# A hybrid decoder trunk on one core: gate and up matrices of the experts in runs of four rows a partition

## What is computed

```python
# mod = silu(c) @ ada_w + ada_b, split into sh1, sc1, g1, sh2, sc2, g2 (1024 channels each)
h = rmsnorm(x, norm2) * (1 + sc2) + sh2
x = x + g2 * hierarchical_moe(h, ...)

def expert_block(xb, e):            # xb: rows of h routed to expert e, of 32
    return (silu(xb @ w1[e]) * (xb @ w3[e])) @ w2[e]
# w1, w3 (gate and up): (32, 1024, 512); w2 (down): (32, 512, 1024)
```

## Time and profile before

| | us |
|---|---|
| median of 3 runs | 1860.86 |
| lowest, highest | 1858.2, 1867.57 |
| the profiled execution | 1862.04 |
| its span, first to last instruction | 1860.0 |
| PE busy in the span | 1669.9 (90%) |
| ACT, DVE busy | 411.1, 602.9 |
| first to last fetch of an expert's matrix issued | 1229.4 to 1799.7 |

### The profile page before, as it was taken

The page is one execution under the profiler, slowest core; times in us unless marked ns, Lnnn a source line. Parts: engine busy times, 40 slices in busy tenths (PEclk is TensorE's granted clock), DMA queues, the critical chain, the costliest instruction groups (busy, mean ns, idle before and its releaser), DMA issues. The chain is left out here.

```text
span 1860.0 us, 33711 instructions
## 1 busy us (share of the span) xinstructions
PE 1669.9 (90%) x14367; PEld 1118.3 (60%) x14367; DVE 602.9 (32%) x1534; ACT 411.1 (22%) x931; POOL 198.4 (11%) x228
## 2 busy tenths in 40 slices
PE   5999999998999979899999899828999988898892
PEld 3444446997777767544444345527777776677672
DVE  3523231004666656665564212260001000000002
ACT  4000000004666646301001011202212212121212
POOL 1205000000110110000000111111111111111110
PEclk9899999999999989999999999868999999999996
DMA  9873223401110044334432331159999999999995
GB/s 325 251 222 100 91 68 116 130 1 41 41 31 14 2 139 137 116 117 127 122 99 85 105 125 68 68 204 387 377 378 377 373 366 379 368 375 374 369 361 217
DMA packets 203953, 355.47 MB, mean 191 GB/s; under 512 B 14831, under 2 KB 94295, under 8 KB 203771
## 3 DMA queue, kind: packets, MB, share of 16 engines
q1 hardware_dynamic: 177264, 305.22, 46.1%
q0 software_dynamic: 13392, 27.93, 5.7%
q10 hardware_dynamic: 13148, 20.16, 3.1%
HBM read 321.29 MB, written 46.86 MB: 198 GB/s over the span
## 5 line engine op out<-in xcount | busy, mean ns | idle before, releaser
L2185 PE MATMUL psum<-sb_m_xT,sb_m_ring 128*64 128x64 f32 x4352 | 138.7, 225 | 30.1 <-issue 25.6
L2185 PEld LDWEIGHTS psum<-sb_m_xT,sb_m_ring 128*64 128x64 f32 x4352 | 134.2, 140 | 44.6 <-issue 44.6
L2180 PE MATMUL psum<-sb_m_xT,sb_m_ring 128*128 128x128 f32 x1152 | 135.9, 279 | 9.8 <-DMA sb_m_ring<-in_exp_w_dram 4.4
L2180 PEld LDWEIGHTS psum<-sb_m_xT,sb_m_ring 128*128 128x128 f32 x1152 | 133.2, 195 | 16.9 <-issue 10.7
L2113 DVE TENSOR_TENSOR sb_m_hT<-psum,sb_m_sg 128x128 f32<-128x128 f32 (+1 forms) x64 | 21.9, 341 | 368.4 <-ACT sb_m_sg L1959 368.4
L2193 PE MATMUL psum<-sb_m_ring,sb_m_hT 128*64 128x512 f32 (+1 forms) x416 | 129.0, 597 | 0.0
L1959 ACT ACTIVATE sb_m_sg<-psum 128x128 f32<-128x128 f32 (+1 forms) x64 | 20.3, 318 | 445.8 <-PE psum L2185 253.0
L1643 PE MATMUL psum<-sb_w_o_sb,sb_mT 128*128 128x512 f32 x256 | 113.2, 601 | 3.7 <-PEq L196 3.7
L711 PE MATMUL psum<-sb_vD,sb_room 128*128 128x512 f32 x240 | 104.6, 592 | 0.0
L1947 ACT ACTIVATE sb_m_xT<-psum,sb_mod,sb_modA 128x64 f32<-128x64 f32 (+1 forms) x256 | 84.4, 435 | 57.8 <-PE psum L2171 57.2
L962 ACT ACTIVATE sb_d_probs<-sb_d_probs,sb_d_nmax 128x640 f32<-128x640 f32 (+7 forms) x128 | 93.3, 736 | 4.9 <-DVE sb_d_nmax L1002 4.4
(11 more groups left out here) (304 smaller groups left out, 2319.7 us busy)
## 6 DMA issues: line engine op xcount, KB each, us to landing
sb_m_ring<-in_exp_w_dram SPq DMA_DIRECT2D x78, 2048.0 KB, 22.8
sb_rows<-in_exp_w_dram SPq DMA_DIRECT2D x18, 2048.0 KB, 22.1
sb_g_ada<-in_ada_w_dram SPq DMA_DIRECT2D x16, 1024.0 KB, 5.3
d_qk<-sb_n_b_sel ACTq DMA_DIRECT2D x20, 512.0 KB, 3.1
sb_hold<-in_w_in_dram SPq DMA_DIRECT2D x16, 512.0 KB, 5.1
sb_n_b_sel<-in_w_in_dram SPq DMA_DIRECT2D x10, 512.0 KB, 8.9
sb_room<-in_w_in_dram SPq DMA_DIRECT2D x10, 512.0 KB, 5.3
sb_oT<-d_qk SPq DMA_DIRECT2D x10, 512.0 KB, 8.8
```

Of the source, the lines that this page charges most:

```text
L2180: mm = pe.matmul(k.psum[:, c // 2, col:col + w], views[which][:, kk, c * P:(c + 1) * P], x[:, kk, 0:w], start=(kk == 0), stop=(kk == KD - 1))
L2185: mm = pe.matmul(k.psum[part, c // 2, col:col + w], views[which][:, kk, c * P + w * h:c * P + w * (h + 1)], x[:, kk, 0:w], start=(kk == 0) ...
```

## The change

A gate or up matrix is fetched so that partition p gets rows `512 h + 4 p + q` with q = 0 to 3, for both halves h. Four rows that lie side by side in memory are one run of 8 KB, so a partition gets two runs. The buffer is then read as before, as eight slices of 512 floats: slice kk = 4h + q holds in partition p the row `512 h + 4 p + q`. The tokens have to follow: the transposes take, for slice kk, the 128 channels `512 h + q + 4 p` of the gathered row, at a step of four floats, and the modulation needs its factors in the same order. They are made once, in `stage_out`: PE turns the two sets of eight columns into rows, ACT copies them out of PSUM, SyncE writes them to DRAM as `d_mod` and reads them back in the new order as `rowmod`. Down matrices are fetched as before. Router logits still use the old order.

```diff
+        self.rowmod = self.sbuf(ctx, "rowmod", [P, 2, KD])
...
+        self.d_mod = dram("d_mod", (2, D))
...
+        s_cols, s_rowmod, s_modT = k.sem("h_mod_stored"), k.sem("h_mod_rows"), k.sem("h_mod_turned")
+        modT = sb("modT", [KD, 2, P])
...
+            sp.wait_ge(s_modT, 2)
+            for i in range(2):
+                sp.dma_start(k.d_mod[i].rearrange("(k p) -> k p", p=P), modT[:, i, :]).then_inc(s_cols, 16)
+            sp.wait_ge(s_cols, 32)
+            for i in range(2):
+                sp.dma_start(k.rowmod[:, i, :].rearrange("p (h q) -> p h q", h=2),
+                             k.d_mod[i].rearrange("(h p q) -> p h q", h=2, p=P)).then_inc(s_rowmod, 16)
             for t in range(NT):
                 sp.wait_ge(s_xn, t + 1)
                 sp.dma_start(k.d_xn[t * P:(t + 1) * P, :], xn[t % 2]).then_inc(s_store[t % 2], 16)
...
             sp.wait_ge(s_sum, 16 * NT)
+            sp.wait_ge(s_rowmod, 32)
...
+            for i, cols in enumerate((k.modA[:, 1, :], k.mod[:, 24:24 + KD])):
+                tr = pe.transpose(k.psum[0:KD, 7, i * P:(i + 1) * P], cols, k.ident)
+            tr.then_inc(s_modT, 1)
             pe.wait_ge(s_wo, 32)
...
+            act.wait_ge(s_modT, 1)
+            act.copy(modT[:, :, :].rearrange("k a p -> k (a p)"), k.psum[0:KD, 7, 0:2 * P]).then_inc(s_modT, 1)
...
+        def expert_weights(w, e, slot, is_down):
+
+            if is_down:
+                return down_w(slot), w[0, bass.ds(e, 1)].rearrange("e (k p) n -> p (e k) n", p=P)
+            return (ring[slot].rearrange("p (h c) -> p h c", h=2),
+                    w[0, bass.ds(e, 1)].rearrange("e (h p q) n -> p (e h) (q n)", h=2, p=P))
...
-                    view = down_w(slot_of(b, i)) if i == 2 else gate_w(slot_of(b, i))
-                    sp.dma_start(view, w[0, bass.ds(e, 1)].rearrange("e (k p) n -> p (e k) n", p=P)
-                                 ).then_inc(s_w[slot_of(b, i)], 16)
+                    sp.dma_start(*expert_weights(w, e, slot_of(b, i), i == 2)).then_inc(s_w[slot_of(b, i)], 16)
...
-                    last = act.activation(dst[:, kk, 0:w], src, ACT.Identity, scale=k.modA[:, 1, kk:kk + 1],
-                                          bias=k.mod[:, 24 + kk:25 + kk])
+                    last = act.activation(dst[:, kk, 0:w], src, ACT.Identity, scale=k.rowmod[:, 0, kk:kk + 1],
+                                          bias=k.rowmod[:, 1, kk:kk + 1])
...
                 for kk in range(KD if w == CAPB else KD // 2):
+                    first = kk // 4 * BANK + kk % 4
                     tr = pe.transpose(k.psum[:, 2 + kk // 4, (kk % 4) * P:(kk % 4 + 1) * P],
-                                      src[:, kk * P:(kk + 1) * P], k.ident)
+                                      src[:, first:first + 4 * (P - 1) + 1:4], k.ident)
```

More of the change, by code:

```diff
@@ L1854, in _ @@
                         for j, w in enumerate((k.exp_w1, k.exp_w3, k.exp_w2)):
[L1855 to L1856 removed]
+                            sp.dma_start(*expert_weights(w, e, j, j == 2)).then_inc(s_ow, 16)
             sp.dma_start(nf, k.norm_f.partition_broadcast(P)).then_inc(s_nf, 16)
```

2 lines of the change are left out of this document (removed).

## The result

The changed kernel takes 1833.06 us at the median of four runs (1829.65 to 1837.04), the kernel before 1861.92 beside it. The ratio is 0.9843, 95% interval 0.981 to 0.9876. Timed again later in five runs it gave 1833.45 us and 0.9848 (0.9834 to 0.9863). The forecast was 1863 us, with a range from 1841 to 1877.

A forecast was written before the change was run, and what follows sets the result against it. With PE and DMA both busy in the expert stage, neither was called the bound; PE's 19.0 us of weight waits framed the gain. -20.6 + 21.6 + 0.3 + 0.9 = +2.2 us gave a 1863 us median, range 1841 to 1877.

The forecast's parts named there:

- The frame: Expert stage: a faster weight stream gains at most PE's 19.0 us of weight waits plus 1.6 us of half clock.
- rival B: Expert stage: PE's instruction blocks arrive later behind 8 KB packets; 1872 us and up, chance 0.17.
- Step 1, packets: Gate and up loads: 8 KB runs at 0.31 us cut DMA time by 45 us, removing weight waits: -20.6 us.
- Step 2, transposes: Turning gathered token rows on PE: 176 transposes load channels at a step of four floats: +21.6 us.
- upper price: Token transposes: each stepped load needs 0.233 us against 0.110, 21.6 us over 176 transposes.
- lower end: Token transposes: a stepped load needs only 0.117 us, so 1 us in all.
- Rival A: Token transposes: the step costs next to nothing, 1842 us; low half of the prices gives 1841 to 1851, chance 0.29.
- Step 3, modulation: ScalarE's modulation reads scale and bias from rowmod, same instructions in the same number: nothing.
- Step 4, rowmod: Making rowmod in the stage before the experts: two more PE transposes count, copy and DMAs are covered: +0.3 us.
- Step 5, gather: First token gather shares DMA engines with 8 KB packets: between 0 and 1.8 us later, taken as +0.9 us.
- Rival C: Gate and up loads: 8 KB may cost four times 2 KB, so weights come no faster; 1866 to 1873 us, chance 0.09.

The follow-up runs named there:

- lighter stream: Kernel before, with down fetches cut from 2 MB to 512 KB from the fourth expert on: 1841.81 us, ratio 0.989.
- the square: Four kernels, transposes with and without the step of four: 1856.29 and 1855.81 us at 2 KB packets, 1833.06 and 1833.36 us at 8 KB.
- order and step, 2 KB: Changed kernel with gate and up fetched in 2 KB packets again, each partition's halves alternating, stepped transposes kept: 1856.29 us, ratio 0.9965.
- order, 2 KB: Changed kernel with gate and up in 2 KB packets, halves alternating, and transposes of neighbouring channels: 1855.81 us, ratio 0.997.
- after, gather first: Changed kernel with SyncE holding the fifth weight load until the first gather has landed: 1833.62 us, ratio 0.987.
- after, two in flight: Changed kernel with each weight load issued only once the load two before it has landed: 1840.36 us, ratio 0.9889.

## Why the prediction was wrong, step by step

**The frame: half right.** "A faster weight stream is worth at most the 19.0 us of waits and what follows from them." The lighter stream measured that part at 22.7 us, near the 20.6. But what follows from the waits was undersized: 1.6 us came from the one stretch at half clock that was read, where the kernel before has four and the clock gave back some 5.3 us by the estimate above. Two of the four stand at stops and not at waits for weights. And the stops named issue did not stay: they fell by 12.2 us, or by 7.7 with the short pauses. The prediction saw that they could change, in rival B, and gave it one sign only.

**Step 1, packets: right.** 0.31 us for 8 KB, no weight waits but 0.3 us, about 410 GB/s forecast for gate and up alone and 2.14 MB in 5 us, 428, measured. 48,576 packets fewer on the page (203,953 to 155,377).

**Step 2, transposes: the term that failed.** +21.6 us forecast, 2.7 us in the timeline, and nothing that a median can tell in the square. The upper price carried the pace of a stepped ordinary load (0.233 us) to a transposing load. The rows had given the lower end too: such a load moves a column as if in half the time. Measured is just that: a step adds 139 ns to an ordinary load (329 - 190) and 70 ns to a transposing one (211 - 141). Little of the 70 ns shows in a row of transposes, whose pace goes from 0.117 to 0.135 us, and the whole costs 2.7 / 176 = 0.015 us a transpose. Rival A, at 0.007 us, was nearer with its 1842 us than the forecast was. The choice went wrong at the sentence on the excess "which a pass that uses a column more quickly does not escape"; the ratio 141 to 192 in the earlier trace rows spoke against it, and that row was of the operation itself. The rule of the Trainium skill that was weighed there (SBUF — State Buffer, Door 1: The DMA port swizzle), read as a price of each line of 16 bytes, would have a step of four floats cost more than a step of two, which falls twice on each line; read as four floats free, it would have neither cost anything. Both loads take 209 to 211 ns here, and that of neighbouring floats 141, so neither reading gives this operand's excess.

**Step 3, modulation: right**, nothing: PE's one wait for it is 3.0 us in both traces. **Step 4, rowmod: the instructions right, the tile missed.** The 3.75 us wait of PE at the start of `stage_out` is now ahead of the two transposes (L1649) and still 3.8 us, and no cost is seen. But the 64 bytes that the tile takes move the ring to a multiple of 128 bytes, worth 6 us at 2 KB and, by a difference whose intervals overlap, 3.6 at 8 KB. The diff showed the tile; no step priced it.

**Step 5, gather: right in kind.** +0.9 us with an end of 1.8; measured 1.6 and, in the second profile, 1.5.

The sum with its failed terms mended, the transposes, the stops (-7.7 in place of nothing) and the rest of the clock (-3.7): -20.6 + 2.7 + 0.3 + 1.6 - 7.7 - 3.7 = -27.4 us, from 1862.0 to 1834.6; measured 1829.65 for the profiled execution, and -28.9 between the medians. The forecast failed by 18.9 us in the transposes and by 11.4 us in stops and clock, both in the same direction.

**Rival B did not come.** It had blocks of instructions arrive later behind packets of 8 KB. The rule of the Trainium skill named with it (DMA: Bandwidth & Descriptors, Queues, rings and completion order) gave an estimate of 57 us slower. No run here shows such a loss: stops and short pauses are 25.6 us at 2 KB and 24.9 at 8 KB with the same rows in the same partitions, and 26.2 at 16 KB. **Rival C fell**: the weights came faster.

**What stays open** is why the stops shortened from before to after. All profiles side by side, in us; the stage is from its first transpose to its last matmul:

| kernel | stops | short pauses | sum | stage |
|---|---|---|---|---|
| before | 31.4 | 0.3 | 31.7 | 570.8 |
| before, again | 32.8 | 0.3 | 33.1 | 570.1 |
| before, 2 idle transposes | 32.9 | 0 | 32.9 | 571.5 |
| before, 66 idle transposes | 28.8 | 0 | 28.8 | 573.7 |
| before, lighter stream | 28.6 | 5.2 | 33.8 | 552.7 |
| before, 64 bytes | 29.6 | 0.3 | 29.9 | 563.5 |
| making of rowmod alone | 24.4 | 4.6 | 29.0 | 565.7 |
| order and step, 2 KB | 22.1 | 4.4 | 26.5 | 565.2 |
| order, 2 KB | 21.1 | 4.5 | 25.6 | 564.9 |
| runs of 4 KB | 22.9 | 5.0 | 27.9 | 549.6 |
| after | 19.2 | 4.8 | 24.0 | 540.5 |
| after, again | 19.8 | 4.5 | 24.3 | 540.5 |
| runs of 8 KB without step | 19.7 | 5.2 | 24.9 | 539.4 |
| after, 64 idle transposes | 24.9 | 0 | 24.9 | 543.2 |
| after, 64 bytes | 25.5 | 0.2 | 25.7 | 541.6 |
| after, ring at 512 | 22.5 | 0 | 22.5 | 537.4 |
| after, gather first | 21.5 | 5.0 | 26.5 | 548.6 |
| after, two in flight | 23.8 | 4.8 | 28.6 | 553.2 |
| runs of 16 KB | 22.7 | 3.5 | 26.2 | 543.3 |

The named stops alone seem to say that rowmod's instructions together with aligned tiles shorten them, and that loss of the alignment brings them back. The sums say neither. They fall from 32 or 33 us to about 30 when the tiles move by 64 bytes, to about 26 when the rows of a matrix also come in the new order, and hardly further with the long runs. Each step of this is one or two executions and 2 to 4 us, two profiles of one kernel differ by up to 1.4, and the 28.8 of the 66 idle transposes does not fit; so it is a description, and not a cause that is shown. Known is that the stops sit at fixed places of the program: counted from the first turning, at the same passes in both profiles of the kernel before, two passes earlier with two idle passes ahead, and 66 earlier with 66, or a block of instructions (127 or 128 passes) further on.

Nor is it shown what makes the short pauses. Every run with about 20 of them was measured on chip 5, 11 or 13, every run without them on chip 10 or 14; the chips of the first two profiles are not on record, and no kernel shows both. The lighter stream has them and differs from the kernel before in nothing that PE executes, and the changed kernel loses them with 64 unused bytes. So a difference of chips is as good an explanation as one of programs, and a comparison of named stops across the two groups is not safe.

At 2 KB the sum hardly matters to the time: 29.9 (64 bytes) and 25.6 (the order) both end at 1856, with 13.4 and 17.4 us of waits for weights. A shorter stop there becomes a longer wait for weights.

## What to carry to other kernels

Read the price of a changed access on the operation that will make it, and where only a neighbour's row has the step, carry the neighbour's ratio to this operation, not its pace. Price every stretch at half clock in the stage, not the longest alone. Before two traces are compared by their named waits, compare the time from the same first to the same last pass: a pause too short to be named can hold what a named one lost. Fetch matrices in runs of 4 to 8 KB a partition where the DMA is full: -15 us at 4 KB and -23 at 8 KB here against 2 KB, and no further gain at 16. When a diff adds or drops an SBUF tile, work out what that does to the start of every big DMA target behind it: 64 bytes were worth 6 us here at 2 KB.

## Unexpected from the hardware

- The place of the tiles in SBUF changes the speed of the stream. With the ring at a multiple of 128 bytes from the first tile it gets 382 GB/s in packets of 2 KB, and 64 bytes off it 377. In the packets' own times, all queues from 1262 to 1500 us, 4 KB took 159 ns at the median against 164, and 8 KB 309 against 312. The whole kernel gains 0.35% (0.23 to 0.48) from an unused tile. All later tiles moved with the ring; the ring's own share isn't measured.
- A transposing weight load takes 141 ns for neighbouring floats and 209 to 211 ns for a step of two or of four floats. With a step of eight in the wide tiles and four in the narrow ones the median is 197.
- At the ends of blocks of PE's instructions (packets of 16 KB) PE stops, for 1.0 to 2.9 us before and 0.5 to 1.8 after, nearly always in narrow experts, whatever the matrices do, and resumes 2.3 to 2.6 us after the packet for the next block starts. With the short pauses the changed kernel still has 24 us of them, its largest remaining loss in this stage.
- Half clock follows stops for instructions too: the lighter stream, with no wait for weights in the stage, has four stretches at 0.50, each at a stop of over 2 us.
